# Moving the split weights and the moving panels of a float32r decoder step by 16 bytes in SBUF

## What is computed

```
x = LN(a*x + 0.5*swiglu(x, ffn1_w_gate, ffn1_w_up, ffn1_w_down))
z = x @ w_in        # q, k, v | conv B, C, h | two gates
o = differential attention (prompt: causal; sample: 1024 cached positions), head norm
y_attn, y_conv = o @ w_attn_out, (c_b * short_conv(c_c * c_h)) @ w_conv_out
x = LN(a*x + (sigmoid(g_attn)*y_attn + sigmoid(g_conv)*y_conv) @ w_o)
x = LN(a*x + 0.5*swiglu(x, ffn2_w_gate, ffn2_w_up, ffn2_w_down))
```

## The kernel before

| panel | matmuls | distance before | distance after |
|---|---|---|---|
| x, all but the first panel pair | 11136 | 144 | 16 |
| x, first panel pair (gate and up chunks in turns) | 384 | 144, 80, 16, 208 | 16, 208, 144, 80 |
| h, first and third panel of an output | 2112 | 144 | 16 |
| h, second and fourth panel of an output | 2112 | 16 | 144 |
| m | 768 | 144 | 16 |
| raw (tiles of 1064 bytes) | 768 | many, steps of 8 | the same + 128 |
| yc | 384 | 16 | 128 |
| o | 384 | 144 | 0 |

## Time and profile before

### The profile page before, as it was taken

One profiled execution on the slowest core, in us unless ns is written; L12 is line 12 of the kernel. 1 busy time (PEld: TensorE's weight loads), 2 busy tenths in 40 slices (PEclk: granted clock), 3 DMA queues, 4 the chain that ended last, 5 costly groups with the idle time before them and its releaser, 6 DMA issues.

```text
span 2272.6 us, 45670 instructions
## 1 busy us (share of the span) xinstructions
PE 2258.4 (99%) x18574; PEld 2227.3 (98%) x18574; DVE 1366.7 (60%) x1523; ACT 998.0 (44%) x1236; POOL 29.8 (1%) x59
## 2 busy tenths in 40 slices
PE   9999999999999999999999999999999999999997
PEld 9999999999999999999998899999999999999997
DVE  5444454444655689999975457886444444445554
ACT  5344444443434454455543454554444444434333
POOL 1000000000000001000000000000000000000001
PEclk9999999999999999999999999999999999999999
DMA  7655555555555688989988855555555555555553
GB/s 247 193 176 184 178 180 180 174 186 183 178 184 179 193 279 289 320 286 328 334 300 317 292 175 190 182 176 185 183 173 187 172 189 178 182 180 181 181 182 116
DMA packets 233439, 475.47 MB, mean 209 GB/s; under 512 B 18448, under 2 KB 21888, under 8 KB 233312
## 3 DMA queue, kind: packets, MB, share of 16 engines
q1 hardware_dynamic: 225920, 465.22, 61.8%
q0 software_dynamic: 2320, 5.68, 0.8%
q10 hardware_dynamic: 5072, 2.78, 0.4%
HBM read 468.13 MB, written 4.43 MB: 208 GB/s over the span
## 4 chain that ended last, share of the span: by engine, by line
PE 99%; POOL 0%; DVE 0%; issue 0%; ACT 0%; DVEq 0%; POOLq 0%
PE ps L651 31%; PE ps L650 31%; PE ps L652 31%; PE ps L764 1%; PE ps L765 1%; PE ps L766 1%; PE ps L907 1%; POOL y L633 0%; PE ps L853 0%; PE ps L795 0%; PE ps L871 0%; PE ps L870 0%; PE ps L877 0%; PE ps L886 0%; PE ps L885 0%; PE ps L884 0%
## 5 line engine op out<-in xcount | busy, mean ns | idle before, releaser
L1382 DVE TENSOR_TENSOR w_lo<-w_raw,w_hi 128x1024 fp32r<-128x1024 f32 x750 | 912.9, 1223 | 799.0 <-ACT w_hi L1004 796.3
L1004 ACT ACTIVATE w_hi<-w_raw 128x1024 fp32r<-128x1024 f32 x750 | 790.4, 1060 | 1022.6 <-PE ps L652 987.6
L652 PE MATMUL ps<-x_hi,w_lo 128*128 128x264 f32 x3840 | 1094.1, 285 | 0.0
L651 PE MATMUL ps<-x_lo,w_hi 128*128 128x264 f32 x3840 | 1092.1, 284 | 0.0
L650 PE MATMUL ps<-x_hi,w_hi 128*128 128x264 f32 x3840 | 1091.5, 284 | 0.2 <-issue 0.2
L650 PEld LDWEIGHTS ps<-x_hi,w_hi 128*128 128x128 f32 x3840 | 726.5, 189 | 12.4 <-issue 8.2
L652 PEld LDWEIGHTS ps<-x_hi,w_lo 128*128 128x128 f32 x3840 | 726.1, 189 | 0.0
L651 PEld LDWEIGHTS ps<-x_lo,w_hi 128*128 128x128 f32 x3840 | 723.5, 188 | 0.0
L651 PE MATMUL ps<-h_lo,w_hi 128*128 128x264 f32 x1408 | 400.8, 285 | 0.0
L652 PE MATMUL ps<-h_hi,w_lo 128*128 128x264 f32 x1408 | 400.4, 284 | 0.0
L650 PE MATMUL ps<-h_hi,w_hi 128*128 128x264 f32 x1408 | 398.7, 283 | 0.0
(11 more groups left out here) (268 smaller groups left out, 1372.3 us busy)
## 6 DMA issues: line engine op xcount, KB each, us to landing
w_raw<-in_ffn_w_down SPq DMA_DIRECT2D x176, 512.0 KB, 3.7
w_raw<-in_ffn_w_gate SPq DMA_DIRECT2D x175, 512.0 KB, 3.5
w_raw<-in_ffn_w_up SPq DMA_DIRECT2D x175, 512.0 KB, 4.3
w_raw<-in_w_in SPq DMA_DIRECT2D x160, 512.0 KB, 5.1
kv_ring<-in_cache_k SPq DMA_DIRECT2D x64, 512.0 KB, 6.0
kv_ring<-in_cache_v SPq DMA_DIRECT2D x64, 512.0 KB, 6.2
w_raw<-in_w_o SPq DMA_DIRECT2D x32, 512.0 KB, 4.2
w_raw<-in_w_conv_out SPq DMA_DIRECT2D x16, 512.0 KB, 5.3
```

The lines of the kernel that those rows point to most:

```text
L651: nc.tensor.matmul(acc, wh, lo[:, kt], start=False, stop=False)
L652: return nc.tensor.matmul(acc, wl, hi[:, kt], start=False, stop=last)
L1004: nc.scalar.activation(w_hi[:, s], w_raw[:, s], ACT.Copy).then_inc(w_hi_ready, 1)
L1382: V.tensor_tensor(w_lo[:, s], w_raw[:, s], w_hi[:, s].bitcast(F32), ALU.subtract).then_inc(w_lo_ready, 1)
```

## The change

The weight rings are allocated first, on a multiple of 128 bytes, without the 16 bytes ahead of them; `w_hi` starts at 16512, `w_lo` at 33152. The panels follow, through a new helper `shifted`, which allocates 16 bytes (`SHIFT` = 4 elements) more and takes the view that begins behind them: the first tile of `x_hi` is at 49808, of `x_lo` at 66704, of `h_hi` at 110736. `w_raw` comes to lie at 83616, which is 32 past a multiple of 128, where it was on one. From `ident` on everything lies where it lay. No instruction is added or removed, and none changes its size.

```diff
-LINE, W_GAP, W_FIRST = 128, 8, 4
+LINE, W_GAP, SHIFT = 128, 8, 4
...
         TILE = N * 4
-        x_at = (top + 31) // 32 * 32
-        x_hi = at("x_hi", [P, DT, N], F32R)
-        x_lo = at("x_lo", [P, DT, N], F32R)
-        y = at("y", [P, DT, N], F32, x_at)
-        y_norm = at("y_norm", [P, DT, N], F32, x_at + DT * TILE)
+        def shifted(name, shape, dt, offset):
+            size = int(np.prod(shape[1:]))
+            flat = at(name, [P, SHIFT + size], dt, offset)[:, SHIFT:SHIFT + size]
+            if len(shape) == 3:
+                return flat.rearrange("p (t n) -> p t n", n=shape[2])
+            return flat.rearrange("p (g t n) -> p g t n", t=shape[2], n=shape[3])
+        SPLIT_RING = RING * KC * (WC + W_GAP)
+        w_at = -(-top // LINE) * LINE
+        def spaced(flat):
+            return flat[:].rearrange("p (s k n) -> p s k n", s=RING, k=KC)[:, :, :, 0:WC]
+        w_hi = spaced(at("w_hi", [P, SPLIT_RING], F32R, w_at))
+        w_lo = spaced(at("w_lo", [P, SPLIT_RING], F32R, w_at + SPLIT_RING * 4))
+        top = w_at + (2 * SPLIT_RING - W_GAP) * 4
+        lam_in = at("lam_in", [HD, 4])
+        x_at = -(-top // LINE) * LINE
+        x_hi = shifted("x_hi", [P, DT, N], F32R, x_at)
+        x_lo = shifted("x_lo", [P, DT, N], F32R, x_at + DT * TILE)
+        y = shifted("y", [P, DT, N], F32, x_at)
+        y_norm = shifted("y_norm", [P, DT, N], F32, x_at + DT * TILE)
+        top = x_at + 2 * DT * TILE + 4 * SHIFT
         w_raw = at("w_raw", [P, RING, KC, WC])
-        lam_in = at("lam_in", [HD, 4])
...
-        w_at = -(-(top + 32) // LINE) * LINE - 32
-            return flat[:, W_FIRST:W_FIRST + SPLIT_RING].rearrange("p (s k n) -> p s k n", s=RING, k=KC)[:, :, :, 0:WC]
-        w_hi = spaced(at("w_hi", [P, W_FIRST + SPLIT_RING], F32R, w_at))
-        w_lo = spaced(at("w_lo", [P, W_FIRST + SPLIT_RING], F32R, w_at + SPLIT_RING * 4))
...
-        h_hi = at("h_hi", [P, FT, N], F32R, area)
-        h_lo = at("h_lo", [P, FT, N], F32R, area + FT * TILE + LINE)
+        h_hi = shifted("h_hi", [P, FT, N], F32R, area)
+        h_lo = shifted("h_lo", [P, FT, N], F32R, area + FT * TILE + LINE)
```

More of the change, by code:

```diff
@@ L133, in program @@
         TILE = N * 4
-        x_at = (top + 31) // 32 * 32
-        x_hi = at("x_hi", [P, DT, N], F32R)
-        x_lo = at("x_lo", [P, DT, N], F32R)
-        y = at("y", [P, DT, N], F32, x_at)
-        y_norm = at("y_norm", [P, DT, N], F32, x_at + DT * TILE)
+        def shifted(name, shape, dt, offset):
[18 more added lines that the diff above has]
+        top = x_at + 2 * DT * TILE + 4 * SHIFT
         w_raw = at("w_raw", [P, RING, KC, WC])
-        lam_in = at("lam_in", [HD, 4])
         lam_prod = at("lam_prod", [HD, 2])
         lam = at("lam", [P, 4])
-        SPLIT_RING = RING * KC * (WC + W_GAP)
-        w_at = -(-(top + 32) // LINE) * LINE - 32
-        def spaced(flat):
-            return flat[:, W_FIRST:W_FIRST + SPLIT_RING].rearrange("p (s k n) -> p s k n", s=RING, k=KC)[:, :, :, 0:WC]
-        w_hi = spaced(at("w_hi", [P, W_FIRST + SPLIT_RING], F32R, w_at))
-        w_lo = spaced(at("w_lo", [P, W_FIRST + SPLIT_RING], F32R, w_at + SPLIT_RING * 4))
-        top = w_at + (W_FIRST + 2 * SPLIT_RING - W_GAP) * 4
         ident = at("ident", [P, P])
@@ L176, in program @@
         area = -(-top // LINE) * LINE
-        h_hi = at("h_hi", [P, FT, N], F32R, area)
-        h_lo = at("h_lo", [P, FT, N], F32R, area + FT * TILE + LINE)
+        h_hi = shifted("h_hi", [P, FT, N], F32R, area)
+        h_lo = shifted("h_lo", [P, FT, N], F32R, area + FT * TILE + LINE)
         h_end = area + 2 * FT * TILE + LINE
-        hid = at("hid", [P, MC, N], F32, h_end)
-        pick = at("pick", [P, GROUPS, HEADS, SEQS], F32, h_end + MC * TILE)
-        raw = at("raw", [P, 2 * DT, RAW], F32R, (h_end - 2 * MC * RAW * 4) // 32 * 32)
+        hid = shifted("hid", [P, MC, N], F32, h_end)
+        pick = at("pick", [P, GROUPS, HEADS, SEQS], F32, h_end + MC * TILE + 32)
+        raw = shifted("raw", [P, 2 * DT, RAW], F32R, (h_end - 2 * MC * RAW * 4) // 32 * 32)
         mean_rstd = mean_sq
-        first_gu = at("first_gu", [P, 2, MC, N], F32, h_end - 5 * MC * TILE)
+        first_gu = shifted("first_gu", [P, 2, MC, N], F32, h_end - 5 * MC * TILE)
         assert h_end - 3 * MC * TILE <= h_end - 2 * MC * RAW * 4
@@ L213, in program @@
         kv_ring = at("kv_ring", [P, PAGE_SLOTS, DC])
-        m_hi = at("m_hi", [P, DT, N], F32R, kv_at)
-        m_lo = at("m_lo", [P, DT, N], F32R, kv_at + DT * TILE)
+        m_hi = shifted("m_hi", [P, DT, N], F32R, kv_at)
+        m_lo = shifted("m_lo", [P, DT, N], F32R, kv_at + DT * TILE)
         assert 2 * DT * TILE <= PAGE_SLOTS * DC * 4
```

## The result

The changed kernel takes **2258.3 us** (median of 6, 2257.48 to 2259.34) against 2274.76 us (2274.2 to 2275.91) of the kernel before in the same comparison: ratio 0.9927, 95% interval [0.9914, 0.994], 16.5 us less. Its profiled execution has a span of 2257.5 us, 15.1 less than before.

The account below looks back on a forecast made before the run. The prediction took back-to-back TensorE matmul spacing as the bound. Its terms, 0 + 0.8 + 0 + 0 = +0.8 us on 2275.51 us, gave 2276.3 us; range 2256 to 2302, or 2273 to 2280 if its mechanism holds.

Parts of the forecast that it names:

- What bounds it: Whole kernel: back-to-back TensorE matmuls set its length, 121.3 ns apart in x, and the spacing depends on tile addresses.
- x, h and m, taken as 0: 16512 matmuls of these panels: new distances and 16-byte starts cost nothing, bounded by -16.5 us and +23 or +69 us.
- The second half: x, h, m: moving tiles 16 past a multiple of 32 with weights on one, the reverse of before, change nothing.
- The lower bound that the step had set down: x, h, m: -1.0 ns per matmul, from two chunks of the first panel pair at 120.2 ns; -16.5 us.
- yc and o, +0.8 us: 768 matmuls with unshifted moving tiles, both tiles now on multiples of 32: +1 ns each, bounds -0.8 to +3.2 us.
- raw, splits, DMAs, ends, taken as 0: Raw panel, weight splitting, weight landings and the last 14 us: no change, with 1 us either way for the ends.
- The slower one: x, h, m: moving tiles touch 34 pieces of 32 bytes instead of 33; 2299 us, at most +61 us; chance 0.27.
- The faster rival: Weights on the line load in 16 pieces for 17, or new places lose the feature-tile surplus; 2259 us; chance 0.23.
- What would show it: Signs: 121.2 ns in both h halves if right; x, h, m wider if slower; all panels closer if faster.
- The check "yc and o included": Sign of the faster rival: the yc and o panels get closer too, as their weights also begin on the line.
- the covers: Spare time hiding splits and weight DMAs: ScalarE waits 1.3 us per chunk for TensorE, landings have over 4 us spare.

Follow-up runs that it names:

- on/16: Moving tiles begin on a multiple of 32 bytes, weights 16 bytes past one: the places of the kernel before, 2274.76 us.
- 16/on: Moving tiles begin 16 bytes past a multiple of 32, weights on one: the places of the changed kernel, 2258.3 us.
- The two runs at distances 0 and 128: Changed kernel with both tiles starting on multiples of 32 bytes (SHIFT = 0), 2278.87 us; then with both starting 16 bytes past, 2266.17 us.
- on/on: Moving and weight tiles both begin on a multiple of 32 bytes; the changed kernel with SHIFT = 0 has this, 2278.87 us.

## Why the prediction was wrong

**What bounds it**: right. Matmul spacing is the kernel's length, it depends on addresses, and the gain came from there alone.

**x, h and m, taken as 0**: this step failed. It was split in two. The first half, that distances 144 and 16 do the same, was read from the earlier trace rows and was true at on/16 (121.25 at 16 in the run with the kernel before at that distance), but at 16/on they differ by 0.3 ns: a comparison at one pair of places was carried over to another. The second half was the reason: "if two streams hinder each other through where each is at the same moment, moving both starts by 16 bytes changes nothing between them", backed by tiles running through starts 32 bytes apart. The two runs at distances 0 and 128 show that moving both by 16 changes 121.7 to 120.6 and 120.1 to 120.9. The rows only ever showed steps of 32. The term was 16512 x 0; measured it was 16512 x about -1.1, less the wait in the mixer: -15 us. The lower bound that the step had set down, -1.0 ns from the earlier trace rows, was the answer almost exactly, since 120.0 is where every pair of places tried ends when its surplus at the change of feature tile is gone.

**yc and o, +0.8 us**: the size was small and right to be small, but +1 ns fits neither. In its last twelve chunks o went from 121.4 to 121.9 ns; its second and third chunk went from 124.0 to 121.8, and the panel as a whole took the same time. yc went the other way, from 121.2 to 120.1 in the chunks near its end that nothing disturbs, and its stretch is 0.1 us shorter.

**raw, splits, DMAs, ends, taken as 0**: right. raw +0.1 us; splits 1059 and 1223 ns; landings within 0.5 us, with the slot cycle's spare time unused; from the start of TensorE's last matmul to the end of the span 12.1 us in both.

**The rivals.** The slower one (an extra piece of 32 bytes per moving tile) did not happen: the tiles that begin 16 past are the fast ones. Its doubt was well placed one step further down, at 8 bytes. The faster rival had the time, 2259 for 2258.3 measured, and half of the mechanism: "the new places lose the surplus after each change of feature tile that distance 80 lacks" is what the start times show, and the kernel before at distance 80 confirms the comparison it was priced from. Its other half, weights on the line, is wrong: on/on with distance 0, 32 or 160 is at 121.7, slower than the kernel before, and of the two panels that were to get closer with it only yc did, o not. The chance of 0.23 for it was too low, since the nearest row to the new places was no nearer to 121.2 than to 120.2, and the sum took the rows of the same distance for the nearer. The range of 2256 to 2302 held the time only because it took in the faster rival; the forecast's own range of 2273 to 2280 did not.

**What would show it** had been put so that it could fail: spacing in both halves of h. It did fail. The check "yc and o included" separated the faster rival's two halves: o, whose weights begin on the line too, did not get closer. Waits of TensorE in the mixer had been named as what would undo the covers; they came on the values of the cached pages and not on the splits, which had not been listed as work that TensorE, being faster, would run into.

## What to carry to other kernels

Where matmuls stand back to back, read the spacing from start times and counts, panel by panel, and compare it with the lowest spacing that the trace holds anywhere: here 1.1 of 121.2 ns, 0.7% of the kernel, lay in addresses alone, and 64 bytes of padding in the old layout would have had it as well as the rewrite. Don't reason the effect of an address from a relation that the trace has only at some places; try the few starts in steps of 16 and 64 bytes, since one run with several panels at different starts measures several at once, and keep starts on 16 bytes. When the bounding engine gets faster, look where work at fixed steps (here page values) waits for something that does not.

## What was not expected of the hardware

- TensorE's spacing with 264 moving columns of float32r and 128 weight columns goes down to 120.0 ns at 2.4 GHz and not under it, at any of the places tried; the surplus of 0 to 1.7 ns is paid in the three or four matmuls after each change of feature tile, or spread in a pattern of 116 to 127 ns.
- Moving both operands by 16 bytes at an unchanged distance changes the spacing by up to 1.6 ns (distance 32: 121.7 with both on a multiple of 32, 120.1 with both 16 past); a distance that is good with one pair of places (80 at on/16, 120.1) is bad with another (80 at 16/on, 121.1).
- A moving tile that starts 8 bytes off a multiple of 16 (distances 8 and 136) costs 2.6 ns or more per matmul, 41 us here.
- Halving the weight load of one matmul in three leaves the 120.1 of x as it is, and changes the surplus of other panels (second h panel +0.3, o -0.95 ns); cutting two of three from 264 to 240 columns gives 13.6 of the 20 ns that 48 columns would be at one per tick of 2.4 GHz.
